# Two-block transformer stack on one core: FFN and out-projection with stationary activations and 512 moving weight columns

## Chip, cores, metric

One core of a Trainium2 chip runs the whole program. The metric is the device time of one execution in microseconds. PE is the matrix engine, PEld its weight loads, DVE the vector engine, ACT the scalar engine, POOL the GpSimd engine and SP the engine that issues the large transfers.

## What is computed

A sequence of 256 tokens with 1024 features passes two blocks of two layers each; all arithmetic has to be close to float32. The mixing of a layer (neighbourhood attention and gated linear attention in the first block; forgetting attention, dilated attention and HGRN2 in the second) is the same work in both kernels. What the change rewrites is the rest:

```python
def rmsnorm(x, g):
    xf = x.astype(jnp.float32)
    y = xf * lax.rsqrt(jnp.mean(xf * xf, axis=-1, keepdims=True) + EPS)
    return (y * g.astype(jnp.float32)).astype(x.dtype)

def swiglu(h, w_gate, w_up, w_down):
    return (jax.nn.silu(h @ w_gate) * (h @ w_up)) @ w_down
...
    x = x + 0.5 * swiglu(rmsnorm(x, ffn1_norm), ffn1_wg, ffn1_wu, ffn1_wd)
    h = rmsnorm(x, mix_norm)
    proj = h @ w_in
...
    x = x + jnp.concatenate([na_o, gla_o], axis=-1) @ w_out
    x = x + 0.5 * swiglu(rmsnorm(x, ffn2_norm), ffn2_wg, ffn2_wu, ffn2_wd)
```

The hidden width of a feed-forward network (FFN) is 2816 = 11 groups of 256. There are two FFNs a layer, so 8 in all, and after each block a final norm.

## The kernel before

**Precision.** Every float32 matrix is split into two float32r parts, hi and lo. A product is three matmuls: hi by hi, hi by lo, lo by hi. ACT writes `w_hi` (L594), DVE subtracts to get `w_lo` (L866), both for a weight unit of 128 x 2048 (1 MB). 332 units pass through the kernel: 33 per FFN, 12 or 14 per layer for the input projection, 4 per layer for the out-projection.

**Weight streams.** Three slots, each with its own stream in HBM, two raw buffers, one hi and one lo buffer. SP loads a raw buffer when its lo part has been made (L249); ACT splits into a slot when PE has used it up (`used`).

**Layout.** The residual `x` is feature-major: 8 chunks of 128 features by 256 tokens. In an FFN the weights are stationary and the 256 tokens move. `column_unit` (L349) makes 256 columns of gate or of up as two halves of a PSUM bank, with 48 matmuls of 128x128 by 128x256. `row_unit` (L359) adds 256 rows of the down projection to four accumulator banks `PD`, again 48 matmuls. A third user of `column_unit` is the input projection; where a result is wanted token-major there, the activations are stationary and 256 weight columns move.

**FFN.** PE runs gate(0), up(0), gate(1), up(1), down(0), then in a loop gate(g), up(g), down(g-1). The rms factor of a token lies along the free axis, so it is a tile `rs` that DVE multiplies in. Per group DVE does L921 (gate by rs), L926, L927, L929 (reciprocal of 1 + exp), L931, L935 and L940 (lo part of the activations); ACT does the exponential L635 and the hi part L642.

**Entering an FFN.** ACT makes `h_hi` from x (L622) and DVE `h_lo` (L899), chunk by chunk; PE fills the wait with 14 matmuls on a zero tile (L369, `keep_awake`). The mean square is summed by DVE and one ones-matmul (L402). Four more matmuls on a zero tile clear the accumulators (L364).

**Entering the mixing.** Here the norm is finished first: ACT squares (L599), PE sums with a ones-matrix (L375), ACT takes the root (L609, L611), DVE scales (L879), ACT and DVE split (L605, L876). PE first computes the small `codes` product (L515), then the input projection.

**Program form.** The layers of a block and the groups of an FFN are loops on every engine, with buffer numbers in registers. At the start, the tables of angles and the lower bounds are computed on DVE and ACT ahead of the first unit.

## Time and profile before

| | |
|---|---|
| time, median of 3 runs (range) | 2288.98 us (2287.17 to 2290.28) |
| span of the profiled execution, first to last instruction | 2281.4 us |
| PE busy | 2191.0 us, 96% |
| PE weight loads busy | 2100.2 us, 92% |
| DVE busy | 1769.9 us, 78% |
| ACT busy | 990.3 us, 43% |
| moved from HBM | 354.77 MB, 156 GB/s over the span |

The span lies 7.6 us below the median of the runs; the page gives no other time of that execution. The page cuts the span into 40 slices of 57 us and gives per slice the busy tenths of each engine, the granted clock of PE and the bytes moved. Its chain of waits (section 4) follows the end of the program back to what released each step. A busy PE is not yet a PE at its peak: matmuls overlap, so their rate is read from the starts in the timeline.

### The profile page before, as it was taken

How to read it: one execution, taken by the hardware profiler on the slowest of the kernel's cores; microseconds unless marked ns; L12 is line 12 of the kernel's file. 1: busy time of each engine (PE TensorE's matmuls, PEld its weight loads, DVE VectorE, ACT ScalarE, POOL GpSimd, SP SyncE). 2: the span in 40 equal slices, each digit the busy share in tenths (PEclk: the TensorE clock that was granted, in tenths of full speed). 3: DMA queues.
4: the chain of work that ended last, by engine and by line, in shares of the span. 5: the costliest groups of instructions: out<-in, count | busy, mean ns of one | idle time of the engine just before them, and what ended most of it. 6: DMA issues, size and time to landing. Idle time of an engine off the chain costs nothing.

```text
span 2281.4 us, 44799 instructions
## 1 busy us (share of the span) xinstructions
PE 2191.0 (96%) x17544; PEld 2100.2 (92%) x17544; DVE 1769.9 (78%) x1769; ACT 990.3 (43%) x1050; POOL 49.1 (2%) x56
## 2 busy tenths in 40 slices
PE   7999989999999999999899999999999999989998
PEld 6999879999999898999899988899989998879998
DVE  7877787877888696878788877678778787777786
ACT  4333564333433455433433353543344335354332
POOL 4000003000000000000000000000000000000000
PEclk9999999999999999999999999999999999899999
DMA  9454326454454433454354432244444543324541
GB/s 302 174 189 166 112 93 179 166 195 155 185 184 165 148 112 121 180 189 165 129 200 168 181 127 100 93 167 165 183 158 185 190 169 130 111 75 150 199 168 37
DMA packets 51214, 357.32 MB, mean 157 GB/s; under 512 B 6480, under 2 KB 6912, under 8 KB 8352
## 3 DMA queue, kind: packets, MB, share of 16 engines
q1 hardware_dynamic: 47952, 349.20, 41.7%
q0 software_dynamic: 2288, 5.25, 1.1%
q10 hardware_dynamic: 864, 1.39, 0.2%
q8 instruction: 70, 1.15, 0.2%
q14 instruction: 40, 0.33, 0.0%
HBM read 354.77 MB, written 1.05 MB: 156 GB/s over the span
## 4 chain that ended last, share of the span: by engine, by line
PE 83%; DVE 9%; issue 3%; ACT 2%; DVEq 2%; ACTq 0%; DMA 0%
PE bank L349 51%; PE bank L359 26%; DVE w_lo L866 2%; PE bank L435 1%; PE bank L375 1%; DVEq L1064 1%; DVE x L890 1%; PE bank L476 1%; DVE arena L1026 1%; DVE arena L976 1%; DVE arena L929 1%; PE bank L515 1%; DVE h_lo L899 1%; PE bank L479 0%; DVE stat L1188 0%
## 5 line engine op out<-in xcount | busy, mean ns | idle before, releaser
L349 PE MATMUL bank<-h_hi,w_hi 128*128 128x256 f32 x3392 | 972.5, 287 | 27.5 <-DVE h_lo L899 19.5
L349 PE MATMUL bank<-h_lo,w_hi 128*128 128x256 f32 x3392 | 965.4, 285 | 0.0
L349 PE MATMUL bank<-h_hi,w_lo 128*128 128x256 f32 x3392 | 965.1, 285 | 0.0
L866 DVE TENSOR_TENSOR w_lo<-raw,w_hi 128x2048 fp32r<-128x2048 f32 x332 | 753.6, 2291 | 161.9 <-ACT w_hi L594 160.4
L594 ACT ACTIVATE w_hi<-raw 128x2048 fp32r (+1 forms) x332 | 632.2, 1906 | 239.7 <-PE bank L349 187.7
L349 PEld LDWEIGHTS bank<-h_hi,w_hi 128*128 128x128 f32 x3392 | 656.6, 194 | 39.9 <-DVE h_lo L899 21.6
L349 PEld LDWEIGHTS bank<-h_lo,w_hi 128*128 128x128 f32 x3392 | 657.1, 194 | 0.2
L349 PEld LDWEIGHTS bank<-h_hi,w_lo 128*128 128x128 f32 x3392 | 656.7, 194 | 0.0
L359 PE MATMUL bank<-act_hi,w_hi 128*128 128x256 f32 x1280 | 363.9, 284 | 0.0
L359 PE MATMUL bank<-act_lo,w_hi 128*128 128x256 f32 x1280 | 362.3, 283 | 0.0
L359 PE MATMUL bank<-act_hi,w_lo 128*128 128x256 f32 x1280 | 362.3, 283 | 0.0
L929 DVE RECIPROCAL arena<-arena 128x512 f32<-128x512 f32 x88 | 295.0, 3353 | 6.5
L359 PEld LDWEIGHTS bank<-act_hi,w_hi 128*128 128x128 f32 x1280 | 245.7, 192 | 1.1
L359 PEld LDWEIGHTS bank<-act_lo,w_hi 128*128 128x128 f32 x1280 | 245.7, 192 | 0.2
L359 PEld LDWEIGHTS bank<-act_hi,w_lo 128*128 128x128 f32 x1280 | 245.7, 192 | 0.0
L635 ACT ACTIVATE arena<-scratch 128x512 f32<-128x512 f32 x88 | 55.7, 633 | 351.6 <-DVE scratch L921 351.6
L642 ACT ACTIVATE act_hi<-scratch 128x512 fp32r<-128x512 f32 x80 | 50.5, 631 | 285.5 <-PE bank L359 270.7
L359 PE MATMUL bank<-h_hi,w_hi 128*128 128x256 f32 x384 | 110.8, 289 | 0.9 <-DVE h_lo L1154 0.9
L359 PE MATMUL bank<-h_lo,w_hi 128*128 128x256 f32 x384 | 109.8, 286 | 0.0
L359 PE MATMUL bank<-h_hi,w_lo 128*128 128x256 f32 x384 | 109.7, 286 | 0.0
L921 DVE TENSOR_TENSOR scratch<-bank,rs 128x512 f32<-128x512 f32 x88 | 60.7, 690 | 62.6 <-PE bank L349 61.5
L926 DVE TENSOR_SCALAR arena<-arena 128x512 f32<-128x512 f32 x88 | 37.6, 427 | 61.5 <-ACT arena L635 61.5
(194 smaller groups left out, 2046.2 us busy)
## 6 DMA issues: line engine op xcount, KB each, us to landing
raw<-stream SPq DMA_DIRECT2D x332, 1024.0 KB, 4.8
arena<-rpb POOLq DMA_DIRECT2D x32, 96.0 KB, 9.3
x<-xt ACTq DMA_DIRECT2D x1, 1024.0 KB, 6.7
out<-x SPq DMA_DIRECT2D x1, 1024.0 KB, 3.9
arena<-c_level POOLq DMA_DIRECT2D x1, 896.0 KB, 10.0
arena<-c_att POOLq DMA_DIRECT2D x1, 512.0 KB, 8.3
arena<-code_w POOLq DMA_DIRECT2D x2, 128.0 KB, 5.0
scratch<-positions ACTq DMA_DIRECT2D x1, 128.0 KB, 2.7
```

What stands on the lines that cost most here:

```text
L349: last = mm(o, a, r, start=(k == 0 and j == 0), stop=(k == KC - 1 and j == 2))
L359: last = mm(o, a[:, w], r, start=False, stop=final and k == 1 and j == 2 and c % 2 == 1)
L375: last = mm(PX[0][:, 0:T], ones, h[:, k, :], start=(k == 0), stop=(k == KC - 1))
L435: last = mm(PD[o][:, at * P:(at + 1) * P], src[rows, 1, ch, j * P:(j + 1) * P], src[rows, 0, ch, tt * P:(tt + 1) * P], start=True, stop=True)
L476: last = mm(o[:, 0:T], aq[rows, hp, q], ak[rows, hp, :], start=True, stop=not fox)
L594: fn(w_hi[s][:, :], raw[s][:, bass.ds(n % RAW, 1), :].rearrange("p a n -> p (a n)"), ACT.Copy).then_inc(hi_done[s], 1)
L635: fn(gate_e, scratch[:, 0, :], ACT.Exp, scale=-1.0).then_inc(eg_ready, 1)
L642: fn(group_parts(g)[0].rearrange("p a b -> p (a b)"), scratch[:, 1, :], ACT.Copy).then_inc(ahi_ready, 1)
L866: tt(w_lo[s][:, :], raw[s][:, bass.ds(n % RAW, 1), :].rearrange("p a n -> p (a n)"), w_hi[s][:, :].bitcast(F32), ALU.subtract).then_inc(lo ...
L921: tt(two(scratch[:, 0, :]), two(banks[0][:, :]), rs2, ALU.mult).then_inc(gate_ready, 1)
L926: ts(gate_e, gate_e, 1.0, None, ALU.add)
L929: v.reciprocal(gate_e, gate_e)
```

## The change

It rewrites the FFNs, the out-projection, the norms and the program's form.

- **Operands swapped.** In FFN and out-projection the activations are stationary (128 features by 128 tokens) and 512 weight columns move (`wide`). A gate/up unit holds 256 gate and 256 up columns of four feature chunks (`front`) or of the other four (`back`); each token tile of 128 has one PSUM bank, gate in its left half, up in its right. The down projection and the out-projection write token-major sums (`row`) into the four banks `PD`. 24 matmuls a unit in place of 48. The input projection stays as it was.
- **Token-major residual.** x is 2 token tiles by 1024 features. The rms factor is one number per partition, `rms`, made of sums that ACT accumulates while it squares (`squares`), one DVE add and a root on 128x2. PE turns x with transposes into PSUM (`turn`), ACT and DVE take `h_hi` and `h_lo` straight from there, with the gain. Before the mixing x is first scaled into `xn` and then turned.
- **Activations turned.** The FFN's product comes out token-major and is turned by 4 transposes a group (`turn_act`), from which `act_hi` and `act_lo` are taken.
- **Gate.** ACT computes the sigmoid straight from PSUM with rms as scale (2 of 128x256 a group), DVE does two operations per token tile. Exponential and reciprocal are gone. ACT changes its function table twice in each FFN.
- **One weight stream.** One stream, 5 raw buffers, 3 slots, units in the order of use. A unit is split as soon as the unit three places ahead of it has been used.
- **Entry and end.** The last unit of an FFN or out-projection finishes one piece of x after the other (`last_row_unit`), and DVE updates it while PE goes on. The zero-tile matmuls are gone. The codes product takes float32r hi and lo parts (96 matmuls in place of 64 half-rate float32 passes). The result leaves in four transfers.
- **Unrolled.** No loops are left. The tables of angles are computed inside the first FFN (groups 2, 4 and 6).

```diff
-RAW = 2
+SLOTS, RAW = 3, 5
...
-raw = [sb(f"raw{s}", [P, RAW, UNIT]) for s in range(3)]
-w_hi = [sb(f"w_hi{s}", [P, UNIT], F32R) for s in range(3)]
-w_lo = [sb(f"w_lo{s}", [P, UNIT], F32R) for s in range(3)]
-x = sb("x", [P, KC, T])
+raw = [sb(f"raw{s}", [P, UNIT]) for s in range(RAW)]
+w_hi = [sb(f"w_hi{s}", [P, UNIT], F32R) for s in range(SLOTS)]
+w_lo = [sb(f"w_lo{s}", [P, UNIT], F32R) for s in range(SLOTS)]
+x = sb("x", [P, 2, D])
...
+def load(u):
+  if u >= RAW:
+    sp.wait_ge(lo_done, u - RAW + 1)
+  sp.dma_start(raw[u % RAW][:, :], stream[u, :, :]).then_inc(raw_ready[u % RAW], 16)
...
-def row_unit(s, chunks_hi, chunks_lo, final=False):
-  for k in range(2):
-    for c in range(KC):
-      w = slice(k * D + c * P, k * D + (c + 1) * P)
-      o = PD[c // 2][:, (c % 2) * T:(c % 2 + 1) * T]
-      for j, (a, r) in enumerate(((w_hi[s], chunks_hi[:, k, :]), (w_hi[s], chunks_lo[:, k, :]), (w_lo[s], chunks_hi[:, k, :]))):
-        last = mm(o, a[:, w], r, start=False, stop=final and k == 1 and j == 2 and c % 2 == 1)
...
-def keep_awake():
-  for _ in range(AWAKE):
-    mm(PX[1][:, :], zero[:, :], square[:, :, :].rearrange("p a b -> p (a b)").bitcast(BF16), start=True, stop=True)
...
+def wide(o, a_hi, a_lo, w, u, start, stop):
+  hi, lo = w_hi[u % SLOTS], w_lo[u % SLOTS]
+  return products(o, [(a_hi, hi[:, w]), (a_hi, lo[:, w]), (a_lo, hi[:, w])], start, stop)
+def gate_up(banks, u, t, kk, k):
+  tok = slice(t * P, (t + 1) * P)
+  return wide(banks[t][:, :], h_hi[:, k, tok], h_lo[:, k, tok], slice(kk * 512, kk * 512 + 512), u, k == 0, k == KC - 1)
+def row(u, i, kk, a_hi, a_lo, start, stop):
+  t, half = i % 2, i // 2
+  tok = slice(t * P, (t + 1) * P)
+  return wide(PD[i][:, :], a_hi[:, kk, tok], a_lo[:, kk, tok], slice(kk * D + half * 512, kk * D + half * 512 + 512), u, start, stop)
...
+def turn(nn, source, half, t):
+  for c in range(4):
+    k = 4 * half + c
+    last = nc.tensor.transpose(XB[k // 2][:, (k % 2) * T + t * P:(k % 2) * T + (t + 1) * P],
+                 source[:, t, k * P:(k + 1) * P], ident)
+    if t == 1 and c % 2:
+      last.then_inc(xt_ready, 1)
+def last_row_unit(u, a_hi, a_lo, nn, following):
+  ready(u)
+  for i in range(4):
+    for kk in range(2):
+      last = row(u, i, kk, a_hi, a_lo, False, kk == 1)
+    last.then_inc(used if i == 3 else acc_done, 1)
+    if following is not None and i == 2:
+      v = following
+      wait_x(pe, v, 1)
+      turn(nn + 1, x, 0, 0)
+      turn(nn + 1, x, 0, 1)
+  if following is not None:
+    wait_x(pe, following, 2)
+    turn(nn + 1, x, 1, 0)
...
+  def front(banks, g):
+    u = ffn_use(b, L, j, "front", g)
+    ready(u)
+    if g >= 2:
+      pe.wait_ge(a_ready, 2 * ffn_no(b, L, j, g))
+    for kk in range(4):
+      if g == 0 and kk % 2 == 0:
+        pe.wait_ge(hlo_ready, 4 * nn + kk // 2 + 1)
+      for t in range(2):
+        last = gate_up(banks, u, t, kk, kk)
+      if g == 0 and kk == 0:
+        wait_x(pe, v, 3)
+        turn(nn, x, 1, 1)
+    last.then_inc(used, 1)
+  def back(banks, g):
+    u = ffn_use(b, L, j, "back", g)
+    ready(u)
+    for t in range(2):
+      for kk in range(4):
+        if g == 0 and t == 0 and kk % 2 == 0:
+          pe.wait_ge(hlo_ready, 4 * nn + 2 + kk // 2 + 1)
+        last = gate_up(banks, u, t, kk, kk + 4)
+      last.then_inc((tile_ready, used)[t], 1)
+  def turn_act(g):
+    pe.wait_ge(a_ready, 2 * ffn_no(b, L, j, g) + 2)
+    for t in range(2):
+      for c in range(2):
+        last = nc.tensor.transpose(PT[:, c * T + t * P:c * T + (t + 1) * P], act[:, t, c * P:(c + 1) * P], ident)
+    last.then_inc(at_ready, 1)
...
+  front(PD, 0)
+  back(PD, 0)
+  for g in range(1, GROUPS):
+    front(PB, g)
+    turn_act(g - 1)
+    back(PB, g)
+    down(g - 1, (lambda: turn_act(GROUPS - 1)) if g == GROUPS - 1 else None)
+  pe.wait_ge(alo_ready, ffn_no(b, L, j, GROUPS - 1) + 1)
+  following = x_no(b, L, 3) if j == 1 and L + 1 < LAYERS else None
...
+def squares(v, pieces):
+  for i in pieces:
+    wait_x(act, v, i)
+    fn(h[:, 2 * i:2 * i + 2, :].rearrange("p a b -> p (a b)"), piece(x, i), ACT.Square, scale=1.0 / 32, accum_out=ssq[:, i // 2, i % 2:i % 2 + 1])
+def turned_hi(b, L, j, pieces):
+  nn = norm_no(b, L, j)
+  for i in pieces:
+    act.wait_ge(xt_ready, 4 * nn + i + 1)
+    if j == 2:
+      act.wait_ge(used, mix_use(b, L, len(MIX[b]) + (UNITS_OUT if i == 1 else UNITS_OUT - 1)))
+    for c in range(2):
+      k = 2 * i + c
+      ins = fn(h_hi[:, k, :], XB[i][:, c * T:(c + 1) * T], ACT.Copy, scale=gain(b, L, ("ffn1", "mix", "ffn2")[j], k))
+    ins.then_inc(hhi_ready, 1)
...
+  def gates(g):
+    for t in range(2):
+      if t == 0:
+        act.wait_ge(tile_ready, ffn_no(b, L, j, g) + 1)
+      else:
+        act.wait_ge(used, use_of("back", g) + 1)
+      src = (PD if g == 0 else PB)[t][:, 0:256]
+      fn(gate_s[:, t, :], src, ACT.Sigmoid, scale=rms[:, t:t + 1]).then_inc(sig_done, 1)
+  def act_high(g):
+    act.wait_ge(at_ready, ffn_no(b, L, j, g) + 1)
+    fn(act_hi[g % 2][:, :, :].rearrange("p a b -> p (a b)"), PT[:, :], ACT.Copy).then_inc(ahi_ready, 1)
...
+  squares(v, [0, 1])
+  turned_hi(b, L, 2 * j, [0, 1])
+  squares(v, [2, 3])
+  turned_hi(b, L, 2 * j, [2, 3])
+  if (b, L, j) == (0, 0, 0):
+    split(use_of("back", 0))
+  root(x_no(b, L, 2 * j))
+  split(use_of("front", 1))
+  table(SIGMOID_SET)
+  split(use_of("front", 0) + SLOTS)
+  gates(0)
+  split(use_of("back", 0) + SLOTS)
+  for g in range(1, GROUPS):
+    act_high(g - 1)
+    split(use_of("front", g) + SLOTS)
+    gates(g)
+    split(use_of("back", g) + SLOTS)
+    if g == GROUPS - 1:
...
-  def gated(banks, g):
-    dve.wait_ge(eg_ready, ffn_no(b, L, j, g) + 1)
-    ts(gate_e, gate_e, 1.0, None, ALU.add)
-    tt(two(scratch[:, 0, :]), two(scratch[:, 0, :]), rs2, ALU.mult)
-    dve.drain()
-    v.reciprocal(gate_e, gate_e)
-    dve.drain()
-    tt(gate_e, gate_e, scratch[:, 0, :], ALU.mult)
-    dve.drain()
-    s, n = ffn_use(b, L, j, "up", g)
-    dve.wait_ge(used[s], n + 2)
-    tt(scratch[:, 1, :], gate_e, banks[1][:, :], ALU.mult).then_inc(a_ready, 1)
+  def gated(g):
+    no = ffn_no(b, L, j, g)
+    banks = PD if g == 0 else PB
+    for t in range(2):
+      dve.wait_ge(sig_done, 2 * no + t + 1)
+      stt(gate_s[:, t, :], banks[t][:, 0:256], rms[:, t:t + 1], gate_s[:, t, :], ALU.mult, ALU.mult)
+      dve.drain()
+      if no and t == 0:
+        dve.wait_ge(at_ready, no)
+      stt(act[:, t, :], banks[t][:, 256:512], rms[:, t:t + 1], gate_s[:, t, :], ALU.mult, ALU.mult).then_inc(a_ready, 1)
+  def act_low(g):
+    dve.wait_ge(ahi_ready, ffn_no(b, L, j, g) + 1)
+    hi, lo = (a[g % 2][:, :, :].rearrange("p a b -> p (a b)") for a in (act_hi, act_lo))
+    tt(lo, PT[:, :], hi.bitcast(F32), ALU.subtract).then_inc(alo_ready, 1)```

How this changes the order on the engines is seen in two places. The first is DVE in one group of an FFN. Names: `bank0`, `bank1` hold the two halves or tiles of a group, `bank6` the turned activations, `raw`, `w_hi`, `w_lo` a weight unit. Before, the loop body up to the second split:

```order
L921 TENSOR_TENSOR scratch<-bank0,rs 128x512 [waits used0]
L925 ISA
L926 TENSOR_SCALAR arena<-arena 128x512 [waits eg_ready]
L927 TENSOR_TENSOR scratch<-scratch,rs 128x512
L929 RECIPROCAL arena<-arena 128x512
L931 TENSOR_TENSOR arena<-arena,scratch 128x512
L934 ISA
L935 TENSOR_TENSOR scratch<-arena,bank1 128x512 [waits used1]
L865 ISA
L866 ISA [waits hi_done0]
L866 TENSOR_TENSOR w_lo0<-raw0,w_hi0 128x2048
```

Now, group 1 of the first FFN:

```order
L988 TENSOR_TENSOR act_lo0<-bank6,act_hi0 128x512 [waits ahi_ready]
L942 TENSOR_TENSOR w_lo2<-raw0,w_hi2 128x2048 [waits hi_done]
L979 SCALAR_TENSOR_TENSOR scratch<-bank0,rms,scratch 128x256 [waits sig_done]
L983 SCALAR_TENSOR_TENSOR scratch<-bank0,rms,scratch 128x256 [waits at_ready]
L979 SCALAR_TENSOR_TENSOR scratch<-bank1,rms,scratch 128x256 [waits sig_done]
L983 SCALAR_TENSOR_TENSOR scratch<-bank1,rms,scratch 128x256
L942 TENSOR_TENSOR w_lo0<-raw1,w_hi0 128x2048 [waits hi_done]
L942 TENSOR_TENSOR w_lo1<-raw2,w_hi1 128x2048 [waits hi_done]
```

Six gate operations of 128x512 became four of 128x256, and a split now stands between the lo part of the activations and the gate operations of the next group.

The second place is PE where the out-projection of the first layer ends and the second FFN begins. `bank5` takes the last products, `square` holds the identity, `x` the residual. Before:

```order
L359 MATMUL bank5<-h_hi,w_lo0 128x256
L369 MATMUL bank7<-square,zero 128x512 x14
L331 REGISTER_ALU
L339 ISA [waits lo_done1]
L349 MATMUL bank6<-h_hi,w_hi1 128x256 [waits hlo_ready]
L349 MATMUL bank6<-h_lo,w_hi1 128x256
```

Now:

```order
L372 MATMUL bank0<-square,x 128x128 [waits x_ready]
L372 MATMUL bank0<-square,x 128x128
L372 MATMUL bank1<-square,x 128x128 x2
L372 MATMUL bank0<-square,x 128x128 x2
L372 MATMUL bank1<-square,x 128x128 x2
L322 MATMUL bank5<-w_hi0,h_hi 128x512
L322 MATMUL bank5<-w_lo0,h_hi 128x512
L322 MATMUL bank5<-w_hi0,h_lo 128x512
```

The 14 fillers are gone, and 8 of the 16 transposes of x stand ahead of the last six products of the out-projection.

## Rows read from the trace of the kernel before

**Rows 1.** Page, section 4: the chain that ended last.

```profile
PE 83%; DVE 9%; issue 3%; ACT 2%; DVEq 2%; ACTq 0%; DMA 0%
```

**Rows 2.** Timeline of PE, first and last of 45 products: start us, us, line, tiles.

```profile
301.51 0.28 PE L349 MATMUL bank<-w_hi,h_hi 128*128 128x256 f32 x1
...
306.78 0.29 PE L349 MATMUL bank<-w_hi,h_lo 128*128 128x256 f32 x1
```

**Rows 3.** Timeline of PE and its weight loads behind a wait.

```profile
39.67 0.19 PEld L349 LDWEIGHTS bank<-h_hi,w_hi 128*128 128x128 f32 x1 [0.89 <-DVE w_lo L866]
...
39.77 0.19 PEld L349 LDWEIGHTS bank<-h_lo,w_hi 128*128 128x128 f32 x1
39.89 0.28 PE L349 MATMUL bank<-h_lo,w_hi 128*128 128x256 f32 x1
```

**Rows 4.** PE, 512-wide fillers and transposes: durations (min/median/max ns), then timeline.

```profile
L369 PE MATMUL bank<-square,zero x112: 376/379/631, 5.2 to 2075.1; 128*128 128x512 bf16 x112
...
1496.25 3.20 PE L369 MATMUL bank<-square,zero 128*128 128x512 bf16 x14
...
L489 PE MATMUL bank<-square,scratch x128: 270/272/332, 270.5 to 2043.0; 128*128 128x128 f32 x128
...
306.90 0.60 PE L489 MATMUL bank<-square,scratch 128*128 128x128 f32 x4
```

**Rows 5.** Timeline of PE at the lower clock, in the first FFN, 10 products apart.

```profile
20.00 0.41 PE L349 MATMUL bank<-h_hi,w_lo 128*128 128x256 f32 x1
...
22.14 0.42 PE L349 MATMUL bank<-h_hi,w_hi 128*128 128x256 f32 x1
```

**Rows 6.** Windows: us; PE, PEld, DVE, ACT, POOL busy (instructions); clock, DMA share, GB/s.

```profile
917.10:1109.00 191.90, 191.82 (x1590) 191.08 (x1590) 151.99 (x117) 74.69 (x61) 0.00 (x0) 1.00 0.48 175
...
sum 1563.10, PE 1548.39 PEld 1537.01 DVE 1264.55 ACT 626.99 POOL 31.13; mean PE 193.55 PEld 192.13 DVE 158.07 ACT 78.37 POOL 3.89
...
913.30:917.10 3.80, 3.52 (x19) 1.56 (x17) 3.28 (x7) 2.56 (x7) 0.00 (x0) 1.00 0.92 308
```

**Rows 7.** Timeline: last product of an FFN, first of the projection behind it.

```profile
218.81 0.28 PE L359 MATMUL bank<-h_hi,w_lo 128*128 128x256 f32 x1
...
230.78 0.39 PE L349 MATMUL bank<-h_hi,w_hi 128*128 128x256 f32 x1
```

**Rows 8.** Timeline at the end of the first block, from its last product on.

```profile
1108.68 0.28 PE L359 MATMUL bank<-h_hi,w_lo 128*128 128x256 f32 x1
1109.00 2.48 DVE L890 SCALAR_TENSOR_TENSOR x<-bank,x 128x512 f32<-128x512 f32 x4 [7.03 <-PE bank L359]
...
1122.37 0.58 PE L349 MATMUL bank<-h_hi,w_hi 128*128 128x256 f32 x1 [5.22 <-DVE h_lo L899]
```

**Rows 9.** Timeline: first product of all; last product; transfer of the result.

```profile
19.41 0.58 PE L349 MATMUL bank<-h_hi,w_hi 128*128 128x256 f32 x1 [8.94 <-DVE h_lo L899]
...
2267.39 0.28 PE L359 MATMUL bank<-h_hi,w_lo 128*128 128x256 f32 x1
...
2277.14 0.35 SPq L273 DMA_DIRECT2D out<-x  x1
```

**Rows 10.** Groups by line on DVE and ACT: count | busy us, mean ns | idle before.

```profile
L866 DVE TENSOR_TENSOR w_lo<-raw,w_hi 128x2048 fp32r<-128x2048 f32 x332 | 753.6, 2291 | 161.9 <-ACT w_hi L594 160.4 <-issue 1.2
L594 ACT ACTIVATE w_hi<-raw 128x2048 fp32r x252 | 479.9, 1906 | 187.9 <-PE bank L349 182.2 <-PE bank L359 5.7
...
L940 DVE TENSOR_TENSOR act_lo<-scratch,act_hi 128x512 fp32r<-128x512 f32 x80 | 62.0, 775 | 18.4 <-ACT act_hi L642 18.4
...
L642 ACT ACTIVATE act_hi<-scratch 128x512 fp32r<-128x512 f32 x80 | 50.5, 631 | 285.5 <-PE bank L359 270.7 <-DVE scratch L935 14.7
...
L622 ACT ACTIVATE h_hi<-x,par 128x256 fp32r<-128x256 f32 x64 | 26.4, 494 | 37.3 <-DVEq L1333 19.2 <-DVE x L890 18.1
L899 DVE SCALAR_TENSOR_TENSOR h_lo<-x,par,h_hi 128x256 fp32r<-128x256 f32 x64 | 26.0, 477 | 0.0
...
L839 ACT ACT_TABLE_LOAD  x1: 1283/1283/1283, 3.7 to 3.7; - x1
```

More of the change, by code:

```diff
@@ new lines, in row_unit @@
+            def row_unit(u, a_hi, a_lo, first, between=None):
+                ready(u)
+                for kk in range(2):
+                    for i in range(4):
+                        last = row(u, i, kk, a_hi, a_lo, first and kk == 0, False)
+                    if kk == 0 and between is not None:
+                        between()
+                last.then_inc(used, 1)
[6 more added lines that the diff above has]
+                        last.then_inc(xt_ready, 1)
@@ L613, in ffn @@
             def ffn(b, L, j):
-                nn = norm_no(b, L, 2 * j)
-                if j == 0:
-                    split(*ffn_use(b, L, j, "gate", 0))
-                    act.wait_ge(layer_par, layer_no(b, L) + 1)
-                for k in range(4):
-                    act.wait_ge(x_ready, 4 * nn + k + 1)
-                    for c in range(2 * k, 2 * k + 2):
-                        ins = fn(h_hi[:, c, :], x[:, c, :], ACT.Copy, scale=gain(("ffn1", "ffn2")[j], c))
-                    ins.then_inc(hhi_ready, 1)
@@ new lines, in update, with turned_lo @@
+            def update(nn, scale, pieces):
+                for i in pieces:
+                    if i == 3:
+                        dve.wait_ge(used, last_row(nn) + 1)
+                    else:
+                        dve.wait_ge(acc_done, 3 * nn + i + 1)
+                    stt(piece(x, i), PD[i][:, :], scale, piece(x, i), ALU.mult, ALU.add).then_inc(x_ready, 1)
+            def turned_lo(b, L, j, pieces):
+                nn = norm_no(b, L, j)
+                for i in pieces:
+                    dve.wait_ge(hhi_ready, 4 * nn + i + 1)
+                    for c in range(2):
+                        k = 2 * i + c
+                        ins = stt(h_lo[:, k, :], XB[i][:, c * T:(c + 1) * T], gain(b, L, ("ffn1", "mix", "ffn2")[j], k),
+                                  h_hi[:, k, :].bitcast(F32), ALU.mult, ALU.subtract)
+                    ins.then_inc(hlo_ready, 1)
@@ L1334, in _ @@
+            dve.wait_ge(first_loaded, 16 * N_FIRST)
+            split(0)
+            for b in range(2):
+                for L in range(LAYERS):
                     ffn(b, L, 0)
```

736 lines of the change are left out of this document (334 added, 402 removed).

## Prediction

> **What bounds the kernel now.** The reader looks at the chain of waits first: 83% of it is PE, 9% DVE, 2% ACT, no transfer [rows 1]. Then at the windows of the FFNs. In one of them PE is busy 191.82 of 191.90 us at the full granted clock (1.00, that is 2.4 GHz), DVE 152, ACT 75, the transfers half their time [rows 6]. So an FFN is bound by the rate at which PE takes matmuls, and a busy share cannot show that rate. The timeline can: between the first and the last start of [rows 2] lie 44 steps in 5.27 us, 0.120 us a matmul of 256 columns. 1584 such matmuls make 190.1 us, which is the window.
>
> What are the 0.120 us made of? At the lower clock (1.2 GHz) ten steps take 2.14 us, 0.214 each [rows 5]; half of that, 0.107, would be the column rate at full clock, so 0.013 us of each matmul is something else. Behind a wait, the first weight load of 128 columns takes about 0.105 us, until the next one can start, and the following matmul starts 0.12 us after that [rows 3]. So weight load and product go on side by side, are nearly equally long, and the pair costs 0.120. A 512-wide product over the same kind of load has its own row: 14 fillers take 3.20 us, (3.20 - 0.38)/13 = 0.217 each, with a median length of 0.379 [rows 4]. They are bf16; a float32r product with 512 moving columns is in no row.
>
> **The products.** The FFNs hold 8 x 33 x 48 = 12,672 matmuls of 256 columns, the out-projections 4 x 4 x 48 = 768: 13,440 at 0.120 = 1612.8 us. They become 6720 with 512 columns. Bounds for one: 0.214, twice the 0.107 of 256 columns, and 0.240, if float32r columns stream no faster than 256 in 0.120. Between them lies 0.227, if each matmul carries the 0.013 with it. I take 0.216, the filler's, because its columns, its array time and its load are those of the new product, and because a load of 0.105 us is then half as long as the product beside it. 6720 x 0.216 = 1451.5: **-161.3 us**.
>
> The Trainium skill, "TensorE: Matmul & The Clock Gate", section "Wait — 56ns, not 53.3ns?", speaks against so large a gain: back-to-back starts lie N/2.4 + 2.5 ns apart, 109.2 ns at 256 columns and 215.7 at 512. By it the swap saves 2.7 ns a pair, 18 us in all. The trace agrees with it at 512 and not at 256, where it shows 120.
>
> **The transposes.** Four of 128x128 take 0.60 us, (0.60 - 0.27)/3 = 0.109 each [rows 4]. New are 88 groups x 4 and, at six FFN entries, 16: 448 x 0.109 = **+48.8**. Those of the other entries are counted in their places below.
>
> **FFN entries.** The eight FFN windows sum to 1563.1 us [rows 6]; their products are 12,672 x 0.120 = 1520.6. The other 42.5 is waiting, the mean square, clearing and the lower clock. Now PE works through it: 8 transposes run while the last piece is multiplied, `h_hi` and `h_lo` come at about 0.49 and 0.48 us an operation [rows 10], two of each per 2.6 us of products. Left is the latency of the first pair, some 0.5 us six times: **-39.5**. In front of each second FFN of a layer stood 3.8 us of fillers [rows 6], four times: **-15.2**. Clearing before the out-projections, 16 x 0.217: **-3.4**.
>
> **Mixing entries.** From the last product to the first of the projection 11.97 us [rows 7]. Now: update of the last piece 0.3 + 0.7, squares 0.6 and their sum 0.2, add and root on two columns some 1.0, scaling 0.5, four transposes 0.5, then four pairs of `h_hi` at 1.0 us each, `h_lo` and the rest of the codes products 1.9, hand-overs of 0.1 a step: 9.3. Four times **-10.7**.
>
> **Block end, start, tail.** Between the blocks 13.7 us pass [rows 8]. Now the root is there 2.8 us after the last product, four final operations of 0.7 follow, and the first pair is ready at 7.0: **-6.7**. At the start the first product waits until 19.4 us [rows 9] behind tables that move into the first FFN; the first weight unit and x need to have landed and been split, which I put at 12.5: **-7**. Tail: 14.0 us from the last product to the end [rows 9]; now 2.8 + 4 x 0.7 + about 3 for the last small transfer: **-5.2**. Places where PE stands still can be followed by a stretch at the lower clock, where the columns take twice as long [rows 5]; I allow 1.5 us at each mixing entry: **+6**.
>
> **What costs nothing, and its cover.** A group is now 72 x 0.216 + 0.44 = 16.0 us of PE. DVE: three lo parts of 2.29, four gate operations of 0.48, one of 0.78 = 9.6 us; ACT: three of 1.91, two sigmoids near 0.49, one of 0.63 = 7.4 [rows 10]. Both sit beside PE. The chain that could surface: a front unit ends, four transposes 0.4, ACT's hi part 0.6 and split 1.9, DVE's lo part 2.3, then four gate operations 1.9 with drains 0.5, hand-overs 0.4: 8.0 us, and the next front unit needs it after back and down, 0.4 + 5.2 + 5.2 = 10.8. If that cover went, PE would wait at every group. The 16 table loads of 1.28 us [rows 10] lie where ACT has 8 us a group free. A unit of 1.05 MB is wanted every 5.33 us, 197 GB/s against 175 at a share of 0.48 [rows 6], so a share of 0.54. The unrolled program fetches more instructions; no row prices that.
>
> **Sum.** -161.3 + 48.8 - 39.5 - 15.2 - 3.4 - 10.7 - 6.7 - 7 - 5.2 + 6 = -194.2. The span 2281.4 becomes 2087; the median of the runs lies 7.6 above the span, so 2095. Behind a wait a product starts 0.22 us after its first (39.67 to 39.89 in [rows 3]) and not 0.12; if the two switches to and from transposes in a group cost up to half of that extra, 88 x 0.05 = 5 us go on top: **2100 us**.
>
> **Rivals.**
> - *The 0.013 us stay with every product.* For: nothing in a float32r row shows it going away. Against: [rows 3], where load and product compete and a longer product outlasts the load. 6720 x 0.011 = +74: 2174.
> - *Columns stream at 120 ns per 256.* For: the rate is the same with weights or activations stationary. Against: at half the clock 256 columns take 0.214 [rows 5], so the array itself needs 0.107 for them at full clock. The products gain nothing: 2100 + 161 = 2261.
> - *Transposes do not overlap.* Each costs its full 0.272 us: 448 x 0.163 = +73, 2173. Against: [rows 4]. The Trainium skill, the same page, "Part 4: PE-mode transpose", measures about 275 ns for one in a kernel and says that transposes do not bring the clock up. The trace agrees with 272 as length, but starts them 0.109 apart.
> - *The ring becomes the bound, and it is slower than before.* One hand-over chain on two in-order engines feeds PE's next front unit. For: gates, splits and turned parts now alternate in one queue, and a front unit waits for both token tiles. Against: 2.8 us of room. It decides beyond 10.8 us of chain; to lose against before it must reach 13.1, 5.1 more than worked out. Then a group takes 18.3 us and the kernel 2100 + 88 x 2.3 = 2302.
> - *The change does not do what it says:* excluded, the order of PE has the 512-wide products.
>
> **Chances.** Forecast 0.60, products at 0.227 0.18, no gain in the products 0.07, long transposes 0.04, the ring 0.05, a smaller loss by waits that I did not see 0.06. The range takes in the first two and the transposes, with 35 us below the forecast for entries and start that I priced by sums of small steps: 2065 to 2195. About 0.2% is what a measurement can tell from no change here. Faster by more than that 0.94, within it 0.01, slower 0.05.
>
> **What would show it.** In the FFN windows: about 176 to 178 us each in place of 192 to 199; starts 0.216 apart in the timeline of PE; PE's weight loads far below its products in busy time, since there are half as many; DVE near 105 of 177 us. Mixing entries near 9 us, FFN entries without a wait over 1 us. Starts 0.227 or 0.240 apart would name the first or second rival. Waits of the first product of a front unit on DVE's gate operations, once a group, would name the ring. The prediction is wrong if the windows are right and the sum is not, or if PE waits for DVE within the groups.

## The result and the profile after

The changed kernel takes 2204.61 us (median of 4 runs, 2204.07 to 2210.44) against 2288.07 for the one before on the same chip: 0.9638 of its time, 95% interval 0.9622 to 0.9654. The sign was forecast, the size was not: 2100 us lies 105 us lower, and the range ended at 2195. The profiled execution has a span of 2202.1 us against 2281.4, a gain of 79.3 us where the sum on record had 189.2. The medians lie 83.5 us apart, 4 more than the spans. The forecast added 7.6 us from span to median; in the profiled run after the two differ by 2.3 (2204.4 against 2202.1), and in the later runs of the kernel before by 2 to 3, so its profiled execution was some 5 us faster than the median.

The page of the changed kernel: busy times, the chain of waits, and the costliest groups of products (columns as in [rows 1, 10]).

```profile
span 2202.1 us, 26811 instructions
PE 2110.0 (96%) x11128; PEld 1781.5 (81%) x11128; DVE 1359.0 (62%) x1565; ACT 1048.5 (48%) x1242; POOL 46.9 (2%) x58
...
PE 84%; DVE 8%; ACT 4%; issue 2%; DVEq 1%; ACTq 1%; DMA 0%
...
L322 PE MATMUL bank<-w_hi,h_hi 128*128 128x512 f32 (+1 forms) x1792 | 690.1, 385 | 20.5 <-DVE h_lo L1209 16.1
```

PE still sets the end, with about the same share of the chain as in [rows 1]. So the time is again the number of products times their rate, and the timeline of PE gives that rate. Inside a group of the second FFN:

```profile
399.70 0.39 PE L322 MATMUL bank<-w_lo,h_hi 128*128 128x512 f32 x1
...
401.29 0.40 PE L322 MATMUL bank<-w_hi,h_lo 128*128 128x512 f32 x1
401.53 0.60 PE L432 MATMUL bank<-square,scratch 128*128 128x128 f32 x4
401.88 0.48 PE L322 MATMUL bank<-w_hi,h_hi 128*128 128x512 f32 x1
```

From 399.70 to 401.29 lie seven steps: 0.227 us a product of 512 columns, against 0.120 for 256 in [rows 2]. Half the products save 0.013 us a pair, not 0.024. The four transposes need 0.59 us from the start of the product ahead of them to that of the next one, 0.36 more than a product alone.

Two of the FFN windows, first product to last (columns as in [rows 6]):

```profile
17.26:217.46 200.20, 190.77 (x839) 156.56 (x840) 122.00 (x124) 92.30 (x88) 22.61 (x25) 0.97 0.61 198
...
1082.74:1270.26 187.52, 187.52 (x840) 155.02 (x840) 106.59 (x98) 83.54 (x80) 0.00 (x0) 0.99 0.51 180
```

In the second one 792 products at 0.227 make 179.8 us, eleven times four transposes 4.0; 3.7 are left, of which 2.5 lie in products at the lower clock behind its start. The forecast had said 176 to 178. The first FFN has another 12.7 us. There the timeline shows what no term of the sum foresaw (DVE, POOL, ACT and one line of PE; the brackets say how long the engine had been idle, and for whom):

```profile
67.06 0.30 DVE L1342 TENSOR_SCALAR arena<-arena 128x256 f32<-128x256 f32 x1
67.44 8.07 DVE L1345 SCALAR_TENSOR_TENSOR arena<-arena 128x256 f32<-128x256 f32 x3
67.92 6.81 POOL L298 TENSOR_TENSOR arena<-arena,col_mask 128x3072 f32<-128x3072 f32 x1 [26.30 <-DMA arena<-rpb]
...
78.09 0.63 ACT L906 ACTIVATE cos_sin<-cos_sin 128x512 f32<-128x512 f32 x1 [13.51 <-DVE cos_sin L1357]
78.73 1.28 ACT L637 ACT_TABLE_LOAD   x1
...
83.37 0.58 ACT L690 ACTIVATE act_hi<-bank 128x512 fp32r<-128x512 f32 x1
...
85.70 0.68 DVE L988 TENSOR_TENSOR act_lo<-bank,act_hi 128x512 fp32r<-128x512 f32 x1
```

```profile
86.44 0.79 PE L322 MATMUL bank<-w_hi,act_hi 128*128 128x512 f32 x1 [8.66 <-DVE act_lo L988]
```

Three DVE operations on 128x256, each some 0.4 us beside their neighbours, last 8.07 us together while POOL adds the masks. ACT waits 13.5 us for the tables, then loads function tables, and only then serves the FFN. PE stands still for 8.66 us, and the first ten products behind that start 0.43 us apart, which costs 2.3 us more.

An FFN entry, once more in the timeline, with the line of DVE that comes ahead of the updates:

```profile
361.45 2.29 DVE L942 TENSOR_TENSOR w_lo<-raw,w_hi 128x2048 fp32r<-128x2048 f32 x1 [3.15 <-ACT w_hi L634]
363.66 1.88 DVE L950 SCALAR_TENSOR_TENSOR x<-bank,x 128x512 f32<-128x512 f32 x3
```

```profile
363.10 0.39 PE L322 MATMUL bank<-w_hi,h_lo 128*128 128x512 f32 x1
365.00 1.09 PE L372 MATMUL bank<-square,x 128*128 128x128 f32 x8 [1.51 <-DVE x L950]
```

Each piece is six products, so the last product of piece 0 started at 360.4 and that of piece 1 at 361.7; but the split of a weight unit comes first in DVE's queue, and it had to wait for ACT's half until 361.45. This occurs at six entries, 1.90 us from start to start each time where 0.23 would be no wait.

**The sum, term by term** (profiled executions; the last products, first products and windows are read as in [rows 6 to 9]; the windows of the six entries begin at the last product ahead of the transposes):

| term | on record | measured |
|---|---|---|
| 6720 wide products for 13,440 | -161.3 | -87.4 (x 0.227) |
| 448 transposes and the switches to them | +53.8 | +42 |
| rest of the FFN windows: entries, fillers, stalls | -54.7 | -17 |
| out-projections apart from products | -3.4 | +5 |
| mixing entries with their lower clock | -4.7 | -5.5 |
| rest of the mixing | 0 | -3.4 |
| block end | -6.7 | -6.0 |
| start | -7 | -2.2 |
| tail | -5.2 | -5.1 |
| sum | -189.2 | -79 |

Of the 110 us between the columns 74 are the first line.

### The profile page after: what moved, and what is told of

Same layout as the page of the kernel before. It is cut to its first block, busy times and chain, and to the rows that moved or that the text cites. A ratio compares the mean times of both kernels' runs of the same rounds, so it can differ in the third digit from the quotient of the medians.

```text
span 2202.1 us, 26811 instructions
## 1 busy us (share of the span) xinstructions
PE 2110.0 (96%) x11128; PEld 1781.5 (81%) x11128; DVE 1359.0 (62%) x1565; ACT 1048.5 (48%) x1242; POOL 46.9 (2%) x58
## 4 chain that ended last, share of the span: by engine, by line
PE 84%; DVE 8%; ACT 4%; issue 2%; DVEq 1%; ACTq 1%; DMA 0%
PE bank L322 76%; DVE w_lo L942 3%; PE bank L432 2%; ACT w_hi L634 2%; PE bank L471 1%; PE bank L372 1%; DVE arena L1033 1%; PE bank L512 1%; DVE x L950 1%; ACT h L643 0%; DVEq L1120 0%; PE bank L515 0%; DVE stat L1248 0%; DMA cos_sin<-positions 0%; PE bank L536 0%
## 5 line engine op out<-in xcount | busy, mean ns | idle before, releaser
L942 DVE TENSOR_TENSOR w_lo<-raw,w_hi 128x2048 fp32r<-128x2048 f32 x332 | 766.4, 2309 | 492.5 <-ACT w_hi L634 492.2
L634 ACT ACTIVATE w_hi<-raw 128x2048 fp32r<-128x2048 f32 x332 | 634.5, 1911 | 284.6 <-PE bank L322 276.3
L322 PE MATMUL bank<-w_hi,h_hi 128*128 128x512 f32 (+1 forms) x1792 | 690.1, 385 | 20.5 <-DVE h_lo L1209 16.1
L322 PE MATMUL bank<-w_hi,h_lo 128*128 128x512 f32 (+1 forms) x1792 | 678.2, 378 | 0.0
L322 PE MATMUL bank<-w_lo,h_hi 128*128 128x512 f32 (+1 forms) x1792 | 677.8, 378 | 0.0
L322 PEld LDWEIGHTS bank<-w_hi,h_hi 128*128 128x128 f32 x1792 | 343.1, 191 | 84.6 <-issue 21.7
L322 PEld LDWEIGHTS bank<-w_hi,h_lo 128*128 128x128 f32 x1792 | 342.8, 191 | 62.6
L322 PEld LDWEIGHTS bank<-w_lo,h_hi 128*128 128x128 f32 x1792 | 343.4, 192 | 57.6
L322 PE MATMUL bank<-w_hi,act_hi 128*128 128x512 f32 x704 | 276.0, 392 | 8.7 <-DVE act_lo L988 8.7
L322 PE MATMUL bank<-w_hi,act_lo 128*128 128x512 f32 x704 | 274.8, 390 | 0.0
L322 PE MATMUL bank<-w_lo,act_hi 128*128 128x512 f32 x704 | 274.7, 390 | 0.0
L690 ACT ACTIVATE act_hi<-bank 128x512 fp32r<-128x512 f32 x88 | 52.7, 599 | 312.9 <-PE bank L432 312.9
L322 PE MATMUL bank<-h_hi,w_hi 128*128 128x256 f32 x576 | 167.8, 291 | 0.4 <-ACT arena L748 0.4
L322 PE MATMUL bank<-h_lo,w_hi 128*128 128x256 f32 x576 | 165.3, 287 | 0.0
L322 PE MATMUL bank<-h_hi,w_lo 128*128 128x256 f32 x576 | 165.2, 287 | 0.0
L988 DVE TENSOR_TENSOR act_lo<-bank,act_hi 128x512 fp32r<-128x512 f32 x88 | 60.8, 691 | 166.2 <-ACT act_hi L690 166.2
L322 PEld LDWEIGHTS bank<-w_hi,act_hi 128*128 128x128 f32 x704 | 132.7, 188 | 36.3 <-DVE act_lo L988 9.1
L322 PEld LDWEIGHTS bank<-w_hi,act_lo 128*128 128x128 f32 x704 | 132.6, 188 | 27.9
L322 PEld LDWEIGHTS bank<-w_lo,act_hi 128*128 128x128 f32 x704 | 132.8, 189 | 27.3
L322 PEld LDWEIGHTS bank<-h_hi,w_hi 128*128 128x128 f32 x576 | 113.0, 196 | 5.0 <-issue 4.2
L322 PEld LDWEIGHTS bank<-h_lo,w_hi 128*128 128x128 f32 x576 | 113.1, 196 | 0.0
```

Source lines behind the costliest of these rows:

```text
L322: last = mm(o, a, r, start=start and n == 0, stop=stop and n == len(pairs) - 1)
L634: fn(w_hi[u % SLOTS][:, :], raw[u % RAW][:, :], ACT.Copy).then_inc(hi_done, 1)
L690: fn(act_hi[g % 2][:, :, :].rearrange("p a b -> p (a b)"), PT[:, :], ACT.Copy).then_inc(ahi_ready, 1)
L942: tt(w_lo[u % SLOTS][:, :], raw[u % RAW][:, :], w_hi[u % SLOTS][:, :].bitcast(F32), ALU.subtract).then_inc(lo_done, 1)
L988: tt(lo, PT[:, :], hi.bitcast(F32), ALU.subtract).then_inc(alo_ready, 1)
```

## The experiments

All edits are to the changed kernel. 2204.6 us is its time; the kernel before ran beside each group, at 2287.8 to 2288.6, and the changed kernel did not run again. The intervals of the ratios to before are 0.001 to 0.003 on either side, 2 to 7 us. So the differences of e4, e5 and e8 to the changed kernel (1 to 4 us) are not told from none by the times; what is said of these runs rests on their traces.

**e1, what the 0.013 us belong to.** Behind the last product, 20 trains of 17 products each (written once here; M and W are the shape):

```diff
+for n in range(17):  # one train a shape
+  mm(PB[n % 2][0:M, 0:W], h_hi_flat[:, stationary(n, M)], w_hi[n % 2][:, 0:W], start=True, stop=True)
```

> The changed kernel with 20 trains of 17 products each behind its last product, on operands left in SBUF, results unused. Starts within a train are read from the timeline. Theory A, every float32r product carries about 13 ns besides its columns, whatever its width: 227 ns at 512 moving columns, 200 at 448, 173 at 384, 147 at 320, 120 at 256, with 128, 64 or 32 stationary columns alike; bf16 trains 216 at 512 and 109 at 256. Theory B, the 13 ns are the weight load of 128 float32r columns that gets in the way of the product: with 64 or 32 stationary columns the same 512-wide product starts every 214 to 216 ns and the 256-wide one every 107 to 110. Rival C, the columns themselves stream slower for float32r than for bf16: the excess over the columns at 2.4 GHz grows with the width (6 ns at 256 against 13 at 512). At 192 and 128 moving columns the load of 105 ns could become the bound: 105 to 120.

Timeline of PE, one merged line a train (start, us from first start to last end):

```profile
2197.61 4.02 PE L628 MATMUL bank<-w_hi,h_hi 128*128 128x512 f32 x17
2201.47 3.61 PE L630 MATMUL bank<-w_hi,h_hi 128*128 128x448 f32 x17
...
2207.89 2.65 PE L634 MATMUL bank<-w_hi,h_hi 128*128 128x320 f32 x17
2210.37 2.20 PE L636 MATMUL bank<-w_hi,h_hi 128*128 128x256 f32 x17
...
2214.28 2.03 PE L640 MATMUL bank<-w_hi,h_hi 128*128 128x128 f32 x17
...
2223.97 4.10 PE L646 MATMUL bank<-w_hi,h_hi 128*32 128x512 f32 x17
...
2229.89 2.10 PE L650 MATMUL bank<-w_hi,h_hi 128*32 128x256 f32 x17
...
2237.97 3.62 PE L656 MATMUL bank<-w_hi,h_hi 128*128 128x512 bf16 x16
...
2244.19 2.02 PE L660 MATMUL bank<-w_hi,h_hi 128*128 128x256 bf16 x17
2246.05 1.11 PE L662 MATMUL bank<-w_hi,h_hi 128*128 128x128 bf16 x17
```

Median steps, float32r: 227 ns at 512 columns, 202 at 448, 174 at 384, 147 at 320, 120 at 256, then a floor of 111 at 192 and 128. Bf16: 216, 162 at 384, 109, 56. The excess over the columns at 2.4 GHz is 13 to 15 ns at the float32r widths from 256 to 512 and 2 to 3 at every bf16 width, so theory A holds in the range that the kernel uses and C falls. With 64 and 32 stationary columns the 256-wide step goes to 117 and 113 (B had 107 to 110), but the 512-wide one to 229 and 231: A had no change at either width, and B is refuted by the second. A repeated stationary operand changes nothing (227, 120).

The trace before already held a difference between the filler and a float32r product: the weight load of the one lasts half as long as that of the other (PEld; count | busy us, mean ns | idle before). The second fence is of e12 below, where bf16 products take 0.225 us.

```profile
L349 PEld LDWEIGHTS bank<-h_hi,w_hi 128*128 128x128 f32 x3392 | 656.6, 194 | 39.9 <-DVE h_lo L899 21.6
...
L369 PEld LDWEIGHTS bank<-square,zero 128*128 128x128 bf16 x112 | 10.9, 102 | 21.9 <-issue 11.4
```

```profile
L322 PEld LDWEIGHTS bank<-w_hi,act_hi 128*128 128x128 bf16 x704 | 67.9, 96 | 99.2 <-DVE act_lo L990 9.1
```

In e12 the load is as short as the filler's and the step is long all the same. So the length of the load is not what costs.

**e2, the width alone.** Each wide product as two of 256 columns:

```diff
-return products(o, [(a_hi, hi[:, w]), (a_hi, lo[:, w]), (a_lo, hi[:, w])], start, stop)
+trio = [(a_hi, hi), (a_hi, lo), (a_lo, hi)]
+for n, (a, r) in enumerate(trio):
+  for q in range(2):
+    cols = slice(w.start + 256 * q, w.start + 256 * q + 256)
+    last = mm(o[:, 256 * q:256 * q + 256], a, r[:, cols], start=start and n == 0 and q == 0, stop=stop and n == 2 and q == 1)
+return last
```

> The changed kernel with each 512-wide product of the FFNs and out-projections done as two of 256 columns on the same stationary activations: 13,440 at 0.120 us in place of 6720 at 0.227. Fixed cost a product (A, or B, since the loads double too): +6720 x (0.240 - 0.227) = +87 us, 2292 us, as slow as the kernel before. Cost by the column (C): 2205 +- 5. My forecast on record took 0.216 for the wide product: by it +161 us, 2366.

2282.34 us (10 runs; 0.9977 of before, 0.9967 to 0.9987): +78 us.

```profile
405.12 0.40 PE L350 MATMUL bank<-w_hi,act_hi 128*128 128x256 f32 x2
405.36 0.40 PE L350 MATMUL bank<-w_lo,act_hi 128*128 128x256 f32 x2
```

A pair takes 0.240. This is the fixed cost at full scale, 78/6720 = 0.012 us a pair where the trains have 0.013 (+87 was expected by them), and it says more: without the width, all the rest of the rewrite is worth 0.2%. Its transposes (42 us) eat what entries, fillers, start and tail give.

**e3, transposes twice over.** `for t in (0, 1, 0, 1)` in place of `range(2)` in `turn_act`.

> The changed kernel with the four transposes of each group's activations done twice over. 352 more transposes. If they start 109 ns apart as in the trace: +38 us, 2243. If each costs its whole length of 272 ns: +96, 2300. If PE had room at that place (the ring of gates and splits is what sets the pace): 0 to +10.

2246.05 us (0.9818 of before, 0.9794 to 0.9842): +41 for 352 transposes, 0.118 each, with 0.10 to 0.14 inside the intervals. They cost their step (0.109), not their length (0.272), and nothing hides them.

**e4, tables at another time.** `TABLES_AT` with groups 5, 7, 9 for 2, 4, 6.

> The changed kernel with the three steps of angle tables inside the first FFN moved from groups 2, 4 and 6 to groups 5, 7 and 9. In the changed kernel PE stands still for 8.7 us in the first FFN, behind a DVE operation that took 8.07 us instead of 1.42 while GpSimd's 6.8 us addition of the masks ran, and then behind table loads and a sine on ACT; 10.2 us at the lower clock follow. Theory: the held DVE operation is harmless unless the tables chain is behind it: -8.7 and -5 us, 2191 us, and the addition now holds up one weight split on DVE (7 us instead of 2.3), which PE's lead covers as it does in the second layer. Rival: the held operation stops PE wherever it falls: 2200 to 2205. Second rival: the tables chain alone (two table loads and a sine in ACT's queue) stops PE: 2200 to 2205, with the stall in group 5.

2200.68 us, runs from 2193 to 2204. The window of the first FFN, then DVE and POOL in the FFN of the next part of the program, and PE:

```profile
18.66:209.57 190.91, 187.59 (x839) 154.16 (x840) 119.91 (x124) 92.29 (x88) 22.70 (x25) 1.00 0.63 206
```

```profile
369.88 6.88 POOL L298 TENSOR_TENSOR arena<-arena,col_mask 128x3072 f32<-128x3072 f32 x1 [12.29 <-DMA arena<-rpb]
370.01 8.90 DVE L942 TENSOR_TENSOR w_lo<-raw,w_hi 128x2048 fp32r<-128x2048 f32 x1 [0.94 <-ACT w_hi L634]
...
380.87 1.11 PE L432 MATMUL bank<-square,scratch 128*128 128x128 f32 x4 [4.31 <-DVE scratch L983]
```

The time lies in the range of both rivals (2200 to 2205) and not at the theory's 2191. The profiled execution was the slowest of the four, 2203.5. In it the first FFN became 9.3 us shorter, of 13.7 expected: more than half of the 10.2 us at the lower clock, which the expectation priced at 5, lie in the stall itself, and the products behind it lost only 2.3. And the second mask addition now met a split just as it began, which then lasted 8.90 us instead of 2.29, and here the gate operations waited behind it and PE for them. In the changed kernel a split begins 3.2 us after the second addition does, lasts 7.05 us and costs PE nothing:

```profile
382.44 7.05 DVE L942 TENSOR_TENSOR w_lo<-raw,w_hi 128x2048 fp32r<-128x2048 f32 x1
```

So a held operation is harmless or not by where in a group it falls, and small shifts elsewhere decide that.

**e8, the addition in eight pieces** of 128x384:

> The changed kernel with GpSimd's addition of the masks (128x3072, 6.8 to 8.1 us in the traces so far) issued as eight additions of 128x384. Theory: a DVE operation that begins while the addition runs is held until it ends; with pieces of about 0.9 us it is held for one piece at most. The three operations of the tables that took 8.07 us take 1.4 to 3, and the first FFN's stall of 8.7 us falls to 2 or 3: its window goes from 200.2 us to 191 to 194, the time to 2195 to 2200. Rival: DVE is held while any of GpSimd's work on that tensor is queued: 8 us again, 2204.

2201.24 us, a little above the 2195 to 2200 of the theory. The three operations took 3.50 us in place of 8.07:

```profile
67.86 8.66 POOL L300 TENSOR_TENSOR arena<-arena,col_mask 128x384 f32<-128x384 f32 x8 [22.45 <-DMA arena<-rpb]
67.96 3.50 DVE L1347 SCALAR_TENSOR_TENSOR arena<-arena 128x256 f32<-128x256 f32 x3
```

So DVE is held by one operation of POOL at a time. But each of the chain's next operations is held a little as well (0.5 to 1.1 us for 0.2 to 0.4), and the stall of PE only fell to 7.0 us, not to 2 or 3; the window is 196.4. The held operation alone does not make the stall: the chain of tables with its table loads does, stretched by POOL.

**e5 and e9, the split ahead of the updates.** First form (e5): behind the updates of pieces 0 to 2. Second form (e9): behind two `h_lo` pairs too, and at every entry; only the lines of an FFN entry are shown.

```diff
 update(nn - 1, (0.5, 1.0)[j], [0, 1, 2])
+split(use_of("back", 0))   # e5
 turned_lo(b, L, 2 * j, [0])
 update(nn - 1, (0.5, 1.0)[j], [3])
-turned_lo(b, L, 2 * j, [1, 2, 3])   # stays in e5
+turned_lo(b, L, 2 * j, [1])   # e9
+split(use_of("back", 0))   # e9
+turned_lo(b, L, 2 * j, [2, 3])   # e9
```

> The changed kernel with the DVE split (2.29 us) that stands ahead of the updates of x at six FFN entries moved behind the updates of pieces 0 to 2. Theory: that split is what makes PE wait 1.9 us before the transposes at each of these entries; the wait falls to 0.3 or less, six times -1.6: 2195 us. Rival: the wait only moves to the first products of the next FFN, since the chain of h_hi, h_lo and the last piece is as long as before: 2202 to 2205.

2203.39 us: the rival was right. The transposes follow without a wait, and the wait stands ahead of the next FFN's first product, behind an `h_lo` that the moved split delays:

```profile
362.65 1.03 PE L372 MATMUL bank<-square,x 128*128 128x128 f32 x8
...
363.46 2.28 DVE L942 TENSOR_TENSOR w_lo<-raw,w_hi 128x2048 fp32r<-128x2048 f32 x1
...
365.65 0.87 DVE L959 SCALAR_TENSOR_TENSOR h_lo<-bank,par_all,h_hi 128x256 fp32r<-128x256 f32 x2
...
366.67 0.47 PE L322 MATMUL bank<-w_hi,h_hi 128*128 128x512 f32 x1 [1.17 <-DVE h_lo L959]
```

> The second form of the late split: at every entry (FFN, mixing, block end, end of the program) the DVE split that stood ahead of the updates of x goes behind them and behind the first two h_lo pairs (at a mixing entry behind all four). The first form stood ahead of the first h_lo pair and moved the wait from 1.9 us before the transposes to 1.44 us before the next FFN's first product. Theory: FFN entries wait 0.3 us or less (six times -1.3), mixing entries 2.1 us instead of 4.0 (four times -1.9, since the squares can start as the pieces finish), block end and tail -1.9 each: 2183 to 2188 us. Rival: ACT's split or its squares are next in the way: 2195 to 2203.

2196.03 us (0.9600 of before, 0.9586 to 0.9615), 8.6 us less where 17 to 22 were expected; it lies in the rival's range (2195 to 2203). At the FFN entries the wait is gone:

```profile
359.38 0.39 PE L322 MATMUL bank<-w_hi,h_lo 128*128 128x512 f32 x1
359.61 1.03 PE L372 MATMUL bank<-square,x 128*128 128x128 f32 x8
360.40 0.48 PE L322 MATMUL bank<-w_hi,h_hi 128*128 128x512 f32 x1
...
361.87 0.60 PE L372 MATMUL bank<-square,x 128*128 128x128 f32 x4
362.36 0.47 PE L322 MATMUL bank<-w_hi,h_hi 128*128 128x512 f32 x1
```

At the mixing entries only 0.6 us went, since the last piece of x is complete only with the last product and its own update, square and root follow one another. In the profiled run the second mask addition stopped PE for another 4.1 us.

**e6, fillers against the lower clock.** Products of a zero tile, 24 at the start, 12 or 14 in the long waits:

> The changed kernel with bf16 products of a zero tile (512 columns) in PE's long waits: 24 at the start, 12 before each mixing entry's transposes, 14 or 12 before each out-projection, 12 at the block end. Theory: the products and transposes behind these waits run at the lower clock because PE stood still; summed over the changed kernel's trace that costs about 18 us, of which the fillers give back most: 2188 to 2194 us. Rival: fillers that outlast the wait or share nothing with the clock: 2203 to 2215.

2190.96 us (0.9584 of before, 0.9568 to 0.9601): -13.7. The time lies in the range of the theory. The mean granted clock rises from 0.978 to 0.988, and the codes product of the first mixing entry now runs at its full rate, from last product to projection 9.8 us in place of 11.6:

```profile
216.32 2.54 PE L329 MATMUL bank<-zero 128*128 128x512 bf16 x11
219.76 1.97 PE L378 MATMUL bank<-square,arena 128*128 128x128 f32 x16 [0.91 <-DVE arena L1231]
```

The 16 transposes there take 3.65 us in the changed kernel and 1.97 here. The change had taken out the `keep_awake` products; it was right that they cover no wait any more, but PE's stops in other places had become longer: ahead of the first out-projection it stood still 4.29 us at a stretch, in place of 2.79 and four products on a zero tile.

**e7, the start.** The engines wait for two of the five first transfers:

```diff
-act.dma_start(dst, src).then_inc(first_loaded, 16)
+act.dma_start(dst, src).then_inc(first_loaded if n < 2 else late_loaded, 16)
```

> The changed kernel, where the engines wait at the start for two of the five first transfers only (identity and parameters); the other three are waited for ahead of the tables. In the changed kernel all engines wait until 12.0 us for the positions, the last of the five. Theory: start 2 to 3.5 us earlier, 2201 to 2203. Rival: the first weight unit and x land as late, 0 to -1.

2197.88 us (0.9607 of before, 0.9589 to 0.9625): -6.7 by the medians, more than expected. In its trace the first wide product starts at 13.5 us in place of 17.3. The start without this edit is not fixed: by when the positions land, the first wide product of the other profiled runs starts at 17.0 to 19.2 (e4, e5, e8 and e12 at 18.7 and later). So the edit is worth 3.5 to 5.7 us at the start.

**e11 and e12, the forecast's product at full scale.** All wide products in bf16, on a constant tile (e11) or on the upper halves of the same float32r elements (e12). Both leave the float32r products out:

```diff
-return products(o, [(a_hi, hi[:, w]), (a_hi, lo[:, w]), (a_lo, hi[:, w])], start, stop)
+return products(o, 3 * [(small[:, 0:P], small[:, :])], start, stop)                     # e11
+return products(o, [(top(a_hi), top(hi[:, w])), ...], start, stop)                      # e12
```

> The changed kernel with every 512-wide float32r product of the FFNs and out-projections replaced by a bf16 product of the same shape on a constant tile: 6720 products of 128x128 by 128x512, same waits, same splits, same updates; the result of those products is left out. Theory: the train of bf16 products starts every 216 ns as in the probe, the other work stays hidden: 2204.6 - 6720 x 0.011 = 2131 us, products 0.216 apart in the FFN windows. That is what the forecast on record took for the product, and the rest of its miss (2131 - 2100 = 31 us) lies in its other terms. Rival: at the faster rate the ring of splits and gates or the transfers set the pace: 2150 to 2200.

> As before, but the bf16 operands are the upper halves of the same float32r tiles (every second 2-byte element), so that PE reads along the same addresses; the products are then coarse ones. If the 11 ns belong to float32r as a format: 0.216 apart and 2131 us. If they belong to reading 4-byte steps from SBUF: 0.227 and 2205 us.

e11: 2128.29 us (0.9304 of before, 0.9275 to 0.9332), e12: 2187.01 (0.9560, 0.9541 to 0.9578). PE in e11, then in e12:

```profile
399.77 2.54 PE L324 MATMUL bank<-small 128*128 128x512 bf16 x11
```

```profile
399.73 0.39 PE L322 MATMUL bank<-w_hi,h_lo 128*128 128x512 bf16 x1
...
401.98 0.39 PE L322 MATMUL bank<-w_hi,h_hi 128*128 128x512 bf16 x1
```

Eleven starts in e11 lie (2.54 - 0.38)/10 = 0.216 apart, in e12 (401.98 - 399.73)/10 = 0.225. With the forecast's rate the kernel takes 2128 us, and no ring of gates and splits stops it. In e12 neither of the two expected outcomes came out exactly, but nearly the second: bf16 elements that are read in steps of 4 bytes keep 9 of the 11 ns, and of the 76 us that e11 gives back e12 gives 18. So most of the cost goes with the access step, and 2 ns are left for the format or something else. Whether it is the stationary or the moving operand's steps was not tried, and why a step costs is not shown.

**e10, together:** second form of the late split, fillers, start, eight pieces, tables in groups 5, 7, 9.

> All together: late split in its second form, fillers (16 at the start, 7 at mixing entries and block end, 16 or 14 before the out-projections), start behind two transfers, mask addition in eight pieces, tables in groups 5, 7 and 9. If the gains add up: -20 for the splits, -12 for the clock, -6 for the start, -9 for the first FFN: 2158 us, range 2153 to 2170. Rival: fillers and shorter waits overlap, so that the fillers now outlast the waits: 2165 to 2180.

```profile
PE 2114.8 (98%) x11230; PEld 1775.4 (82%) x11239; DVE 1350.5 (62%) x1565; ACT 1050.7 (49%) x1242; POOL 59.6 (3%) x73
```

2163.20 us (5 runs, 2163.02 to 2163.48; 0.9455 of before, 0.9442 to 0.9468), 41 us below the changed kernel and faster than both. It lies in the range of the sum (2153 to 2170) and below the rival's (2165 to 2180). The parts sum to -8.6 - 13.7 - 6.7 - 3.9 (e4) - 3.4 (e8) = -36, with intervals of several us each; the 5 us on top were not taken apart. The second mask addition no longer stops PE, as it did in the profiled runs of e4 and e9: two splits beside its eight pieces last 3.07 and 3.15 us. PE is busy 98%.

## Why the prediction was wrong

- **What bounds the kernel:** right. PE's rate does, before and after.
- **The size of one wide product is the step that failed.** The forecast took 0.216 us from a bf16 filler [rows 4] for a float32r product; it is 0.227. The first rival had the step (0.227) and the reason, a cost that stays with every product. What spoke against it on record, that a longer product outlasts its weight load, is refuted by e1: the excess is 13 to 14 ns whether the product has 256 or 512 columns. The row that it rested on [rows 3] shows a load behind a wait, and says nothing of the excess; its 0.105 us are from one load to the next, the load itself lasts 0.19. The filler was also taken because its load is that of the new product, which the trace contradicts (102 against 194 ns), though by e12 that is not the cause. The row for the filler was nearest in shape, but its elements lie 2 bytes apart and those of float32r 4, and by e12 that is most of what counts. Worth 74 us; e11 gives back 76.
- **The rule of the Trainium skill,** "TensorE: Matmul & The Clock Gate", section "Wait — 56ns, not 53.3ns?" (N/2.4 + 2.5 ns): e1 agrees for bf16 at four widths (216, 162, 109, 56) and not for float32r at any. The first disagreement, 120 at 256, was in the trace before, and was the hint that float32r follows another line. The forecast put it into words and still took the 512-wide figure from bf16.
- **Second rival,** no gain from the width: refuted, the gain is 13 ns a pair (e2).
- **Transposes:** 42 us for 54 on record. Step of 0.109 right within what e3 can tell (0.118, 0.10 to 0.14). The Trainium skill, "TensorE: Matmul & The Clock Gate", section "Part 4: PE-mode transpose", gives some 275 ns, which is here the length (272) and not the cost. The third rival is refuted (e3: +41 us, not +96).
- **FFN entries and windows:** the largest miss after the product, some 38 us with fillers. Somewhat more than half can be named. 11 us are the first FFN's stall with the lower clock behind it (8.7 + 2.3); I had moved the tables into the FFN at no cost, and not asked what is queued behind them on ACT. At six entries 1.7 us stood where 0.5 was taken, 7 us in all, because one split lies ahead of the updates in DVE's queue. Behind the two restarts, at the program's start and at the block end, the lower clock costs some 5 us. The rest, about 14 us, was not traced.
- **Out-projections:** clearing cost nothing before, as it lay in a wait; 3.4 us were booked as gained. The wait was as long after (4.3 us from the heads' last product to the first of the out-projection, 4.2 before), and the lower clock behind the four waits cost 7.7 us where it had cost 3.4.
- **Start:** 17.3 us in place of 12.5. All engines wait for the last of five small transfers, the positions, until 12.0 (in other profiled runs until 13.9), and the forecast looked only at the weight unit and x.
- **Mixing entries, block end, tail:** right within 1 us each. For the mixing entry that is in part luck: the steps listed for it add up to 9.7 us before any hand-over, not to 9.3, and the tail's to 8.6, not 8.8.
- **Span to runs:** 7.6 us were added, 2.3 are measured. This hid 5 us of the other misses in the time.
- **The ring:** right. PE waits for DVE's gate operations nowhere in a group while POOL is silent, and in e11, where products start every 0.216 us, neither.
- **Weight loads** were to fall far below the products in busy time; they show 81%. Each lasts some 190 ns after as before; before, they started every 120 ns and overlapped each other, so half as many are busy for nearly as long. That marker was badly chosen.

After the product's size, the terms left 30 us, and the rival's 74 on top of them ended outside the range: it had taken the rival in at its bare price, as if no other term could miss at the same time.

## What to carry to other kernels

Price an instruction by a row of its own element type and access step, not of its shape alone: 11 ns on 6720 products were 74 us. If no row has it, put the bound of the known excess (here 13 ns in every float32r step of the trace) into the forecast and the better value into a rival. And for work that moves into a stage that has room, ask of every in-order queue what stands behind it: the room is per queue and per moment, not per stage.
